# Routing of the sample by tiles, with each tile's dense gates beside the next one's routing

## The reference

```
def peer_ffn(h, w_q, sub_k1, sub_k2, e_down, e_up):       # per block of 128 tokens
    q = (xb @ w_q).reshape(n, 8, 256); q1, q2 = split(q)
    s1 = einsum('nhd,hkd->nhk', q1, sub_k1); s2 = einsum('nhd,hkd->nhk', q2, sub_k2)
    v1, i1 = top_k(s1, 16); v2, i2 = top_k(s2, 16)
    top_s, top_c = top_k(v1[..., :, None] + v2[..., None, :], 16)
    idx = take(i1, top_c // 16) * 128 + take(i2, top_c % 16)
    g = softmax(top_s)
    act = gelu(einsum('nhkd,nd->nhk', e_down[idx], xb))
    return einsum('nhk,nhkd->nd', g * act, e_up[idx])
```

## Time and profile before

| | |
|---|---|
| median of 3 runs | 2955.6 us (2954.28 to 2955.69) |
| the profiled execution | 2953.1 us, span 2951.3 us |
| mean granted clock of PE | 0.917 |
| busy: PE, DVE, ACT, POOL | 2464.2 (83%), 2301.6 (78%), 1153.2 (39%), 1335.0 (45%) |
| HBM read, written | 708.09 MB, 37.75 MB |

### The profile page before, as it was taken

The page is one execution under the profiler, slowest core; times in us unless marked ns, Lnnn a source line. Parts: engine busy times, 40 slices in busy tenths (PEclk is TensorE's granted clock), DMA queues, the critical chain, the costliest instruction groups (busy, mean ns, idle before and its releaser), DMA issues. The chain is left out here.

```text
span 2951.3 us, 39042 instructions
## 1 busy us (share of the span) xinstructions
PE 2464.2 (83%) x12865; PEld 2127.5 (72%) x12865; DVE 2301.6 (78%) x4186; ACT 1153.2 (39%) x1928; POOL 1335.0 (45%) x1058
## 2 busy tenths in 40 slices
PE   6978877199988888979850665899999999999997
PEld 5856767188866667767640554799999998999996
DVE  6465437867569686656898776799999999999998
ACT  4453433133237323332111998333333333333333
POOL 0000001604531333423466320677777787777774
PEclk9989889599989999999965777899999999999998
DMA  4625433137862676736211764999999999999997
GB/s 150 219 104 178 154 128 109 47 115 263 316 212 79 213 279 239 284 114 229 103 45 44 265 229 175 360 400 401 401 399 399 400 401 401 400 398 400 400 400 278
DMA packets 231175, 747.60 MB, mean 253 GB/s; under 512 B 20864, under 2 KB 70192, under 8 KB 214400
## 3 DMA queue, kind: packets, MB, share of 16 engines
q0 software_dynamic: 112256, 408.71, 36.9%
q1 hardware_dynamic: 118784, 337.22, 31.4%
HBM read 708.09 MB, written 37.75 MB: 253 GB/s over the span
## 5 line engine op out<-in xcount | busy, mean ns | idle before, releaser
L1629 POOL DMA_INDIRECT rows<-in_up,now x384 | 588.5, 1533 | 182.6 <-issue 96.5
L186 DVE TENSOR_TENSOR w_lo<-w_raw,w_hi 128x2048 fp32r<-128x2048 f32 x116 | 269.2, 2322 | 341.8 <-ACT w_hi L180 341.2
L145 POOL DMA_INDIRECT row_ring<-in_down,IDX x208 | 281.9, 1355 | 547.9 <-DVE dots L136 509.7
L201 PE MATMUL lin<-w_hi,T_hi 128*128 128x512 f32 x976 | 395.3, 405 | 59.1 <-PEq L606 9.5
L1737 DVE SCALAR_TENSOR_TENSOR Y<-rows,dots,Y 128x1024 f32<-128x1024 f32 x320 | 404.0, 1276 | 14.3 <-DMA rows<-in_up,now 13.3
L202 PE MATMUL lin<-w_lo,T_hi 128*128 128x512 f32 x976 | 391.2, 401 | 0.0
L203 PE MATMUL lin<-w_hi,T_lo 128*128 128x512 f32 x976 | 390.6, 400 | 0.0
L180 ACT ACTIVATE w_hi<-w_raw 128x2048 fp32r<-128x2048 f32 x116 | 221.6, 1912 | 384.4 <-PE lin L203 363.6
L201 PE MATMUL tr<-T_hi,d_hi 128*128 128x384 f32 x1024 | 344.7, 337 | 14.6 <-DVE d_lo L1710 14.6
L203 PE MATMUL tr<-T_hi,d_lo 128*128 128x384 f32 x1024 | 344.8, 337 | 0.0
L202 PE MATMUL tr<-T_lo,d_hi 128*128 128x384 f32 x1024 | 344.1, 336 | 0.0
(11 more groups left out here) (218 smaller groups left out, 4977.4 us busy)
## 6 DMA issues: line engine op xcount, KB each, us to landing
w_raw<-in_wall SPq DMA_DIRECT2D x116, 1024.0 KB, 5.4
shared<-in_downT SPq DMA_DIRECT2D x128, 512.0 KB, 16.3
shared<-in_up SPq DMA_DIRECT2D x128, 512.0 KB, 16.3
dense_gates<-shared SPq DMA_DIRECT2D x12, 2048.0 KB, 7.5
wd<-dense_gates SPq DMA_DIRECT2D x32, 768.0 KB, 28.4
rows<-in_up,now POOLq DMA_INDIRECT x384, 9.8
row_ring<-in_down,IDX POOLq DMA_INDIRECT x208, 6.0
Y<-in_x SPq DMA_DIRECT2D x6, 512.0 KB, 4.8
```

The lines of the kernel that those rows point to most:

```text
L145: pool.indirect_dma_start(self.ring[:, r % self.K, :], None, self.table, bass.IndirectOffsetOnAxis(ap=self.IDX[:, r:r + 1], axis=0)).then_ ...
L186: dve.tensor_tensor(self.lo[:, h % 2], self.raw[:, h % 2], self.hi[:, h % 2].bitcast(F32), ALU.subtract).then_inc(self.lo_done, 1)
L201: pe.matmul(out, lhs[0], rhs[0], start=start, stop=False, skip_group_check=True)
L1629: pool.indirect_dma_start(rows[:, k, :], None, table, bass.IndirectOffsetOnAxis(ap=now[:, j % 2, k:k + 1], axis=0)).then_inc(rows_in[k], 16)
```

## The change

The routing of the sample becomes a function of its own, `routing_and_gates`, which also makes the dense gates; `dense_gates` and its buffers go.

- The units are ordered by tile: first the eight of tiles 1 and 2 by turns, then the four of tile 3, then those of tile 0 (gathered). The scores of all units stay in `G` and in the row ring, which is why all rows must be done before the second half of them is written.
- Picks 0 to 9 run as before, but with no rows. After pick 9 the softmax of tiles 1 and 2 is done and each of picks 10 to 16 is preceded by six octs of stamps (`PER_UNIT`); the last six octs come behind pick 16.
- The stamps' two slots lie in the ring's places 4 and 5 and in `w_hi`. The matmul writes PSUM with a step of four floats, so that ACT's copy reads 512 floats in a row and writes runs of four.
- All 256 rows come before pick 0. Mixer inputs now have 83, self-attention 27, mixer outputs 54, cross inputs 40, cross attention 5, and the sample's last stage 47, of which 22 stand directly ahead of pick 0 (`bg.finish`).
- POOL makes `place` before it issues the stage's rows, and loads `keys` with the other small tensors.
- `experts` has its own buffers for raw weights, and SP issues down, up and gate weights in turns.

```diff
                 for c in range(11):
-                    bg.dve(dve, 4 if c >= 3 else 0)
+                    bg.dve(dve, 5 if c >= 3 else 0)
                     st.split_lo(dve, H + 2 * c + 2)
-                    bg.dve(dve, 4 if c >= 3 else 1)
+                    bg.dve(dve, 5 if c >= 3 else 1)
...
-                    if step % 2 == 1:
+                    if step % 4 != 0:
                         bg.dve(dve, 1)
...
-                        bg.dve(dve, 5)
+                        bg.dve(dve, 6)
...
                 for h in range(2, 10):
-                    bg.dve(dve, 2)
+                    bg.dve(dve, 3 if h % 2 == 0 else 2)
                     st.split_lo(dve, H + h)
                 turn_x.dve(dve)
                 for h in range(10, 14):
-                    bg.dve(dve, 4)
+                    bg.dve(dve, 5)
...
+        order = [(c, t) for c in range(NPC) for t in (1, 2)] + [(c, 3) for c in range(NPC)] + [(c, 0) for c in range(NPC)]
...
+        PER_UNIT = 6
+        AFTER = {2: 3 * PER_UNIT, 3: 7 * PER_UNIT}
...
+                    for x in range(QUADS):
+                        n = i * QUADS + x
+                        pe.wait_ge(gated, n // 2 + 1)
+                        if n >= 4:
+                            pe.wait_ge(bank_free, n - 3)
+                        for k in range(4):
+                            o, slot = x // 2 % 2, 4 * (x % 2) + k
+                            last = pe.matmul(lin[:, n % 4, :].rearrange("p (e t) -> p t e", t=4)[:, k, :], hot2[:, o, slot, :].bitcast(F32),
+                                             hot1[:, o, slot, :], start=True, stop=True, skip_group_check=True)
+                        last.then_inc(bank_ready, 1)
...
+                    act.wait_ge(bank_ready, n + 1)
+                    act.activation(stage[s][:, :, t0:t0 + 4], lin[:, n % 4, :].rearrange("p (e t) -> p e t", t=4),
+                                   ACT.Copy).then_inc(bank_free, 1)
...
+                def stamp(first, count):
+                    for n in range(first, first + count):
+                        i, r = n // OCTS, n % OCTS
+                        if r == 0:
+                            dve.wait_ge(copied, i + 1)
+                        if n >= 2:
+                            dve.wait_ge(bank_ready, 2 * n - 2)
...
+                bg.dve(dve, 6)
+                st.split_lo(dve, H0 + 6)
+                bg.dve(dve, 6)
+                st.split_lo(dve, H0 + 7)
+                bg.finish(dve)
+                for c in range(1, NPC):
+                    pick_experts(2 * c - 2)
+                    if c < NPC - 1:
+                        st.split_lo(dve, H0 + 6 + 2 * c)
+                    pick_experts(2 * c - 1)
+                    if c < NPC - 1:
+                        st.split_lo(dve, H0 + 7 + 2 * c)
+                for r in range(6, 9):
+                    pick_experts(r)
+                shift(0)
+                shift(1)
+                pick_experts(9)
+                finish(0)
+                finish(1)
+                for r in range(10, UNITS + 1):
+                    stamp((r - 10) * PER_UNIT, PER_UNIT)
+                    pick_experts(r)
+                    if r == 12:
+                        shift(2)
+                    if r == 13:
+                        finish(2)
+                shift(3)
+                stamp(7 * PER_UNIT, ND * OCTS - 7 * PER_UNIT)
+                finish(3)
...
-                load_w(0, 0)
-                load_w(0, 1)
+                for b in range(RAW):
+                    sp.dma_start(raw_d[:, b], A["downT"][b]).then_inc(d_in[b], 16)
+                    sp.dma_start(raw_u[:, b], A["up"][b * P:(b + 1) * P, :]).then_inc(u_in[b], 16)
+                    if b < 2:
+                        load_w(0, b)

```

More of the change, by code:

```diff
@@ L138, in dve, with finish @@
             self.done = r + 1
+    def finish(self, dve):
+        self.dve(dve, self.end)
     def pool(self, pool, upto=None):
@@ L1242, in _ @@
                 dve.wait_ge(small_in, 48)
-                for r in rows_of:
-                    last = dve.tensor_tensor(H[:, r, :], G[:, r - q.t0, :], row[:], ALU.mult)
+                for r in range(NT):
+                    last = dve.tensor_tensor(H[:, r, :], G[:, r, :], row[:], ALU.mult)
                 last.then_inc(h_done, 1)
                 def pick_experts(r):
-                    bg.dve(dve, 1)
-                    taken.append(bg.done)
                     rows = []
@@ L1346, in _ @@
                     pool.dma_start(dst, src).then_inc(small_in, 16)
-                bg.pool(pool, max(bg.asked, min(bg.end, taken[0])))
                 pool.wait_ge(small_in, 48)
@@ L1352, in _ @@
                     u = r
-                    bg.pool(pool, min(bg.end, taken[r] + bg.K))
                     if u < UNITS:
@@ new lines, in normed, with scores @@
+                def normed(n, end):
+                    pe.wait_ge(norm.scaled, norm.base + end)
+                    if n < NT:
+                        pe.wait_ge(o_x.freed, NT + n + 1)
+                turn.pe(pe, normed)
+                turn.wait(pe)
+                pe.wait_ge(small_in, 64)
+                made = []
+                def scores(c, t):
+                    i = len(made)
+                    made.append((c, t))
+                    pe.wait_ge(o_q.freed, 4 * (c + 1))
+                    if i >= 2:
+                        pe.wait_ge(s_copied, i - 1)
+                    for j in range(4):
+                        last = pe.matmul(tr[:, i % 2, j * NK:(j + 1) * NK], qT[:, j, t * P:(t + 1) * P],
+                                         subk[:, 4 * c + j, :], start=True, stop=True)
+                    last.then_inc(s_ready, 1)
@@ L1493, in _, with copy @@
-                with act.Fori(0, ND) as i:
+                st.split_hi(act, H0 + 2)
+                act.wait_ge(o_x.ready, NT)
+                st.split_hi(act, H0 + 3)
+                st.split_hi(act, H0 + 4)
+                norm.act(act, before=lambda t: act.wait_ge(o_x.freed, NT + t + 1))
+                turn.act(act)
+                st.split_hi(act, H0 + 5)
+                def copy(c):
+                    for x, t in enumerate(range(NT) if c < NPC - 1 else (1, 2, 3, 0)):
+                        i = c * NT + x
+                        act.wait_ge(s_ready, i + 1)
+                        act.activation(scores_at(c, t).rearrange("p j k -> p (j k)"), tr[:, i % 2, :], ACT.Copy).then_inc(
+                            s_copied, 1)
@@ new lines, in _ @@
+                for c in range(NPC):
+                    if c == 1:
+                        act.wait_ge(h_done, 1)
+                    if c == 3:
+                        act.wait_ge(bg.used, bg.end)
+                    if c >= 1:
+                        copy(c - 1)
+                    st.split_hi(act, H0 + 6 + 2 * c)
+                    for bank, col, _, cb, cols, need in q.features:
+                        act.wait_ge(o_q.ready, 4 * c + need)
+                        if c >= 1:
+                            act.wait_ge(s_ready, NT * c)
+                        act.activation(qT[:, cb, cols], lin[:, bank, col:col + q.n],
+                                       ACT.Copy).then_inc(o_q.freed, 1)
+                    st.split_hi(act, H0 + 7 + 2 * c)
@@ new lines, in _, with soften @@
+                copy(NPC - 1)
+                def soften(i):
+                    t = (*DENSE_TILES, GATHERED)[i]
+                    act.wait_ge(g_shift, i + 1)
+                    act.activation(GATE[:, t, :], GATE[:, t, :], ACT.Exp).then_inc(g_exp, 1)
+                def gate(i, r):
+                    n = i * OCTS + r
+                    act.wait_ge(stamped, n + 1)
+                    for k in range(OCT):
+                        col = OCT * r + k
+                        last = act.activation(hot1[:, r % 2, k, :], hot1[:, r % 2, k, :], ACT.Copy,
+                                              scale=pairs[:, i, 2, col:col + 1])
+                    last.then_inc(gated, 1)
@@ L1494, in _ @@
+                soften(0)
+                soften(1)
+                for i in range(ND):
+                    act.wait_ge(turned, i + 1)
+                    act.activation(pairs[:, i].rearrange("p j n -> p (j n)"), lin[:, 4 + i % 2, 0:3 * P], ACT.Copy).then_inc(
+                        copied, 1)
+                    act.wait_ge(copied, i + 1)
                     for r in range(OCTS + 1):
+                        for late, n in AFTER.items():
+                            if r < OCTS and i * OCTS + r == n:
+                                soften(late)
@@ new lines, in link @@
+                def link(*instructions):
+                    nonlocal links
+                    for x in instructions:
+                        x.then_inc(chain, 1)
+                        links += 1
+                    dve.wait_ge(chain, links)
+                for c in range(2):
+                    bg.dve(dve, 5)
+                    st.split_lo(dve, H0 + 2 * c + 2)
+                    for t in range(NT):
```

(18 more changed lines are left out.)

327 lines of the change are left out of this document (203 added, 124 removed).

## The result

The changed kernel takes 2963.5 us (median of 11 runs, 2961.8 to 2969.3), the kernel before, in as many runs beside it, 2955.7 (2951.9 to 2962.6). The ratio is 1.0027, with a 95% interval of 1.0017 to 1.0036: 8 us slower, between 5 and 11. The prediction was 2961, its likeliest range 2954 to 2969.

The account below looks back on a forecast made before the run. ACT was taken to pace the dense gates before, the two-slot stamp loop after. From 2953.1 us profiled, +16 early, -10.5 in the joined stretch, 0 at the experts' start, plus 2.5 for the median gave 2961; range 2937 to 2990.

Parts of the forecast that it names:

- The joined stretch: From the first pick to the issue of the last store: 422.9 us before, forecast 412.4, a change of -10.5.
- Item 1: 22 rows ahead of pick 0, covered by nothing and mostly at POOL's issue pace: 36 us, bounds 25 and 41.
- Item 2: Picks 0 to 9 without rows, with low splits, a PE wait, softmax of two tiles, transposes and copies: 106.7 us.
- Items 3 and 4: Seven batches of six octs' stamps plus a pick, 200.4 + 29.3 us; then two tile boundaries, 9, and last octs, 31.
- the loop of two slots: Dense octs: each stamp waits for matmuls two octs back; 8.2 us per pair of octs, binding instead of ACT.
- POOL's meeting: Behind each pick, one two-input DVE instruction runs into POOL's product: +1.7 us per batch, 12 over seven batches.
- The unload: ACT's copies from PSUM in the dense gates: two take 1.07 us instead of 1.98; if unchanged, +12 us.
- The early stages: Rows moved ahead into mixer inputs, self-attention, mixer outputs, cross inputs and the new stage's start: +16 us, 10 to 25.
- The start of the experts: First weight loads behind the last store, with SP issuing blocks in turns: 0 us, -5 to +5.
- B: Rival, faster: PE's clock holds, so an oct's matmuls take 2.05 to 2.75 us; 2938 to 2950 us, chance 0.26.
- C: Rival, slower: dense-gate matmuls pay for writing PSUM four floats apart; 2978 to 3019 us, chance 0.08.
- D: Rival, slower: extra rows in mixer inputs make the weights come late; +15 us, 2976, chance 0.12.

## Why the prediction was right, and where only its sum was

**The joined stretch: right in kind, 8 us too dear.** Predicted 412.4 us, measured 404.7. Item 1 was 36, measured 32.2; that nothing covers it was wrong, since leaving the rows out gave back only 21. Item 2 was 106.7, measured 108.7. Items 3 and 4 were 269.7, measured 263.8. From one pick's end to the next the full batches within a tile take 32.3, 34.2 and 34.3, where I had 33.4; the short one 27.6 for 29.3; from the last pick's end to the last store 30.5 for 31. The tile boundaries cost 2 to 3 above a batch (35.8 and 36.5), not 4.5. That the loop of two slots binds, DVE's wait of 48.9 for matmuls shows, and three slots take it away with 34 us. Inside a batch two terms were off in opposite directions. The matmuls of an oct were put at 3.4 and are 128.4 / 48 = 2.68 in the mean, worth 17 x 0.7 = 12 by my count. I had argued from PE's smaller busy share to a clock near 0.70; the share did fall (129.01 of 263.80 us, before 131.97 of 218.90), but the clock stayed, 0.76 against 0.77. POOL's meeting was put at 1.7 a batch, 12 in all; behind pick 10 it is 3.1, and over all stamps it is 135.1 - 96 x 1.22 = 18, so 6 more than I had. The kernel without lookups ran 12 faster, as I had named, but by another way: 17 came back from the stamps and 7 went into longer waits for matmuls and `pairs`. With these terms put right my sum for the stretch would be some 4 us too small; where those went is open.

**The unload: right.** 1.98 to 1.05 for two, and 9.5 us worth where I had 12.

**The early stages: the step that was mis-sized.** I had +16. Six traces have all the early rows (the changed kernel and those with no 22 rows, no lookups, three slots, both of these, and the old unload). From the first low split of the prompt's last stage to the last one ahead of pick 0 they are 23.3 to 30.3 us behind before, 25.7 in the mean. By stage, mixer inputs 0 to 2.7 (predicted 0), self-attention 12 (9.5), mixer outputs 3.0 to 5.4 (4), cross inputs 2.7 to 6.5 (1.5), the new stage's start up to 0.9 (1). Besides, 2.4 to 2.7 lie between the last split of cross inputs and the first of the last stage, where cross attention stands with its five rows as before; I did not have this in the sum. A part of this is scatter: in cross inputs the unfused kernels, where nothing was changed there, are 0 to 5 behind too, and 0 to 1.6 at that handover. The mean less theirs is 21 to 22. The excess over 16 is then 2.5 in attention, some 1.5 in cross inputs, where I let waits of 1 to 2 us cover rows that arrive late, 1 in mixer inputs, and 1 to 2 at the handover. Only the rows' price as a whole was tried by a run; the cause of each of these excesses was not.

**The start of the experts: right.** From the last store to the first product with gate weights it is 30.6 us instead of 32.1, and the rest of the span is 2.9 longer in this trace. From the last store to the end it is 1.4 longer together, 0.3 to 3.8 in the other traces of the fused kernel and -0.7 to 3.8 in the unfused ones, so this is within the scatter.

So the near hit, 2961 for 2963.5, is two errors of 5 to 9 us with opposite signs: +21 to +25 early, -18 in the joined stretch, about +1 behind, against +16, -10.5 and 0. That the sum came out within 3 us is luck; that it came out slower, with the two slots binding, is not. The stated range of 2937 to 2990 also doesn't follow from its own bounds: added up, they give 2916 (-6, -11, -23, -5) to 2987 (+9, +5, +6.5, +5).

**The rivals.** B came in its own terms (an oct's matmuls at 2.68, just under its 2.7), though not by a better clock, which is 0.76 against 0.77 before; its 12 us were offset by POOL's meetings and the early stages. C, PE's writes, is refuted by the kernel with the old order. The Trainium skill's sentence that a pattern which is not contiguous slows matmuls significantly ("PSUM — Partial Sum Buffer", Specifications (TRN2)) does not hold for this one: fp32, 128 columns, a step of four floats, 340 ns against 347. D half came: rows waited up to 6.5 us for their DMA in mixer inputs and the splits' waits were nearly used up, but PE stayed at 135.00 of 135.00, and 0 to 2.7 us were lost in the six traces. Two other kernels with the same 16 rows there lost more: the one with 9 rows fewer in self-attention 5.4, the unfused one with 16 rows moved 5.1, both with gaps on PE (1.4 and 2.15 us), which was D's sign.

**What the change is made of.** The new unload alone, on the kernel before, gives 24.5; the whole change costs 8. So what is left of it, the fusing and the rows that had to be moved for it, costs 32: 21 to 25 for rows ahead of the joined stretch, some 7 inside it, and the rest scatter. There the fused kernel takes 404.7 us and the unfused one with the new unload 398.0, though it has 66 rows in the stretch and the fused one 22; the stamps beside POOL's lookups alone take some 15 of what the missing rows free. The unfused kernel had room for its 48 rows beside ACT's work, while routing, into which the fusing puts the stamps, was DVE's already. With the slots mended the picture turns: three slots and the fusing take 369.5 us for the joined stretch, four slots without it 376.1 (the fused kernel with four was not tried). As a whole the fused one is still 18 slower (2930.6 against 2912.1): what the joined stretch gains by the fusing is less than what the rows ahead of it cost.

## What to carry to other kernels

Before two stages are fused, ask what each is bound by: here the dense gates were bound by a dear copy and by two buffers in a ring, and mending both without fusing gave 44 us. A ring of two in a chain over three engines binds at half the chain's length (here 8.2 us by the count and 4.1 per oct, as the unfused kernel with the new unload measured); a third slot was worth 34 us. A background task costs little only where its host stage waits, and each stage takes only so much: moving the first 8 rows from attention to mixer inputs brought 11 us (some 7 by the stages), the next 8 nothing more, since what attention gave back the weight stream lost.

## What the runs showed of the hardware

- Single VectorE instructions with two SBUF inputs took 2.93, 2.17 and 1.69 us instead of 1.22 while GpSimd ran one 2.95 us product and its sums; with that work gone they took 1.22 to 1.33. A row of before had shown one such meeting; that POOL's sums do it too was new.
- A ScalarE copy from PSUM of 128 x 512 floats takes 580 ns when it writes runs of four floats, and 1068 to 1083 ns when each float is 128 bytes from the next. That is what the 16-byte lines of the Trainium skill ("SBUF — State Buffer", Specifications (TRN2)) would have it do. The matmul that writes PSUM with the step of four paid nothing for it (340 ns against 347).
- PE's granted clock rose as the gaps between its octs closed: 0.77 with an oct every 4.56 us, then 0.90 and 0.93 in the unfused kernels with the new unload (4.1) and with four slots besides (3.6), and the matmul's mean fell from 343 to 306 and 292 ns. That this shortened the kernel further was not tried by itself.
